# Stick-breaking attention: both heads' scores on row halves, weighted values on column halves, and a new order of the stage

## The reference, cut to what matters

```
q = rms_norm_2(heads(q), q_gain); k = rms_norm_2(heads(k), k_gain); v = heads(v)
z = einsum('bhtd,bhsd->bhts', q, k) * scale              # scale = 1/8
mask = s_pos[None, :] < t_pos[:, None]
log_stay = where(mask, log_sigmoid(-z), 0.0)
later = cumsum(log_stay, axis=3, reverse=True) - log_stay # sum over later keys
weight = where(mask, exp(log_sigmoid(z) + later), 0.0)
out = einsum('bhts,bhsd->bhtd', weight, v)
```

## Time and profile before

| | us |
|---|---|
| device time, median of 3 runs | 2165.52 (2161.07 to 2167.31) |
| span of the profiled execution | 2161.0 |
| stick-breaking attention, first z to first matmul that closes the output projection | 1477.9 to 1757.6 |
| PE busy in the span | 2096.7 |
| DVE / ACT / POOL busy | 907.0 / 737.8 / 811.5 |

### The profile page before, as it was taken

One profiled execution on the slowest core, in us unless ns is written; L12 is line 12 of the kernel. 1 busy time (PEld: TensorE's weight loads), 2 busy tenths in 40 slices (PEclk: granted clock), 3 DMA queues, 4 the chain that ended last, 5 costly groups with the idle time before them and its releaser, 6 DMA issues.

```text
span 2161.0 us, 25942 instructions
## 1 busy us (share of the span) xinstructions
PE 2096.7 (97%) x8990; PEld 1648.1 (76%) x8990; DVE 907.0 (42%) x1040; ACT 737.8 (34%) x967; POOL 811.5 (38%) x328
## 2 busy tenths in 40 slices
PE   7999989999998999999999999999999989999999
PEld 4677758888885777787888888886777768888887
DVE  6455454333224343343234443225777764444300
ACT  3333342233223333334233323224454543333211
POOL 3222244444444433332444444443222224444443
PEclk8999999999998999999999999999999999999999
DMA  4111112223221222221222223222111112222322
GB/s 148 49 49 51 58 57 97 97 97 108 94 90 59 94 86 69 97 82 64 93 96 97 97 97 106 94 83 70 47 49 39 49 49 88 97 97 97 106 94 92
DMA packets 48137, 177.31 MB, mean 82 GB/s; under 512 B 5472, under 2 KB 6240, under 8 KB 48096
## 3 DMA queue, kind: packets, MB, share of 16 engines
q1 hardware_dynamic: 46224, 172.62, 23.5%
q10 hardware_dynamic: 1872, 4.13, 0.6%
HBM read 174.63 MB, written 2.10 MB: 82 GB/s over the span
## 4 chain that ended last, share of the span: by engine, by line
PE 86%; DVE 8%; issue 3%; ACT 3%; DMA 0%; DVEq 0%; ACTq 0%; SPq 0%
PE B L261 23%; PE B L262 23%; PE B L266 23%; PE B L678 2%; PE B L668 1%; PE B L672 1%; PE B L669 1%; DVE SPL L1611 1%; PE B L529 1%; PE B L560 1%; PE B L277 1%; PE B L279 1%; PE B L278 1%; PE B L813 1%; PE B L775 1%
## 5 line engine op out<-in xcount | busy, mean ns | idle before, releaser
L408 POOL TENSOR_TENSOR WL<-RAW,WH 128x1024 fp32r<-128x1024 f32 (+1 forms) x304 | 781.7, 2572 | 1326.3 <-PE B L266 861.4
L261 PE MATMUL B<-HH,WH 128*128 128x512 f32 x1624 | 642.3, 396 | 5.7 <-DVE QT L1348 5.7
L262 PE MATMUL B<-HL,WH 128*128 128x512 f32 x1624 | 633.7, 390 | 0.0
L249 ACT CAST WH<-RAW 128x1024 fp32r<-128x1024 f32 (+1 forms) x304 | 333.8, 1098 | 639.3 <-PE B L262 584.6
L266 PE MATMUL B<-HH,WL 128*128 128x512 f32 x1624 | 401.4, 389 | 0.0
L261 PEld LDWEIGHTS B<-HH,WH 128*128 128x128 f32 x1624 | 306.0, 188 | 78.6 <-issue 9.3
L262 PEld LDWEIGHTS B<-HL,WH 128*128 128x128 f32 x1624 | 305.9, 188 | 65.2 <-issue 2.6
L266 PEld LDWEIGHTS B<-HH,WL 128*128 128x128 f32 x1624 | 304.8, 188 | 63.3
L261 PE MATMUL B<-MH,WH 128*128 128x512 f32 x462 | 182.5, 395 | 0.0
L262 PE MATMUL B<-ML,WH 128*128 128x512 f32 x462 | 182.5, 395 | 0.0
L1274 DVE TENSOR_TENSOR U<-B,RB 128x512 f32<-128x512 f32 x66 | 45.6, 691 | 309.4 <-PE B L266 309.4
(11 more groups left out here) (233 smaller groups left out, 2343.8 us busy)
## 6 DMA issues: line engine op xcount, KB each, us to landing
RAW<-in_w_small SPq DMA_DIRECT2D x256, 512.0 KB, 3.2
RAW<-in_w_large SPq DMA_DIRECT2D x48, 704.0 KB, 4.0
X<-in_x_t ACTq DMA_DIRECT2D x4, 512.0 KB, 8.6
out_t<-X SPq DMA_DIRECT2D x8, 256.0 KB, 5.2
DECAY<-in_decay ACTq DMA_DIRECT2D x4, 256.0 KB, 2.5
INV<-in_inv_counts SPq DMA_DIRECT2D x1, 512.0 KB, 9.2
BIAS<-in_bias SPq DMA_DIRECT2D x1, 256.0 KB, 9.1
CS<-in_cos SPq DMA_DIRECT2D x1, 256.0 KB, 9.1
```

The lines of the kernel that those rows point to most:

```text
L249: act.copy(WH[u.s][:, 0:chunks, :], RAW[u.s][:, 0:chunks, :]).then_inc(s_hi, 1)
L261: pe.matmul(bank, wh[:, c, :], xh[:, k0 + c, :], start=(start and c == 0), stop=False)
L262: mm = pe.matmul(bank, wh[:, c, :], xl[:, k0 + c, :], start=False, stop=False)
L408: pool.tensor_tensor(WL[u.s][:, 0:chunks, :], RAW[u.s][:, 0:chunks, :], WH[u.s][:, 0:chunks, :].bitcast(F32), ALU.subtract).then_inc(s_lo, 1)
```

## The change

The two heads are computed together. `z` now issues all eight strips in one go, head 0 and head 1 in turn, each on its 64 rows of the array, into B2, B3 and one half of B4 for head 0, B5, B6 and the other half of B4 for head 1. `values` issues both heads in turn too: v is kept once (VN3, no zeros), a head's 64 columns of it are loaded and its result goes to partitions 64h to 64h+63 of B7. The memset of VZ3 on GpSimd goes. The new values wait for the weights of both heads, and one semaphore count stands for both.

The stage has a new order. On TensorE: unit q, values of pair a - 1, z of pair a, unit k, the first part of unit v (16 matmuls), the sums of head 0, the last 8 matmuls of unit v, the sums of head 1, the transposes. In the last stage both started output units stand ahead of the sums, and head 1's sums get banks of their own (B5, B6, B7). DVE and ACT are reordered to match.

z and values on TensorE:

```
-                def z(h):
-                    hd = a * 2 + h
+                def z():
                     pe.wait_ge(b_qk, a * 2 + 2)
...
+                    if not first_a:
+                        pe.wait_ge(b_arg, a * 6)
+                    for h, sb_, bank, at in ((0, 2, 4, 0), (1, 0, 5, 0), (0, 0, 2, 0), (1, 1, 6, 0), (0, 1, 3, 0),
+                                             (1, 2, 4, 256), (0, 3, 3, 384), (1, 3, 6, 384)):
                         w = t_width(sb_)
+                        r = slice(64 * h, 64 * h + 64)
+                        if h == 1 and bank == 4:
+                            pe.wait_ge(b_z, a * 8 + 1)
+                        pe.matmul(B[bank][:, at:at + w], KT3[r, ap, P * sb_:P * sb_ + P], QT3[r, ap, P * sb_:T],
+                                  start=True, stop=True).then_inc(b_z, 1)
...
+                def values(a, ap):
+
+                    pe.wait_ge(b_w, a * 2 + 2)
+                    pe.wait_ge(b_v, a + 1)
+                    pe.wait_ge(s_m, a + M_BASE[4])
                     for sb_ in range(TB):
                         w = t_width(sb_)
-                        mm = pe.matmul(B[7][:, P * sb_:T], VZ3[:, ap, h, sb_, :],
...
+                        for h in range(2):
+                            mm = pe.matmul(B[7][64 * h:64 * h + 64, P * sb_:T], VN3[:, ap, sb_, 64 * h:64 * h + 64],
+                                           ZS[:, h, T_AT[sb_]:T_AT[sb_] + w], start=(sb_ == 0),
+                                           stop=(sb_ == TB - 1), skip_group_check=True)
```

The sums' waits and the stage on TensorE (`high_part` and `low_part` are the two halves of `use_unit`):

```
                     if h == 0:
-                        pe.wait_ge(b_zs, hd * 4 + 8)
+                        pe.wait_ge(b_zs, a * 8 + 8)
+                    elif j is not None:
+                        pe.wait_ge(b_arg, hd * 3)
                     else:
-                        pe.wait_ge(b_arg, hd * 3)
...
+                        pe.wait_ge(s_m, a + M_BASE[4])
+                        places = LAST_AT
...
-                if a is not None:
-                    z(0)
...
-                        values(1, a - 1, 1 - ap)
-                    z(1)
+                    if not first_a:
+
+                        values(a - 1, 1 - ap)
+                    z()
                     if j is None:
                         start_out(0)
+                        start_out(1)
+                        later(0)
+                        later(1)
+                        values(a, ap)
...
                     head_mean(0)
-                if a is not None:
-                    later(0)
-                if j is not None:
                     pe.wait_ge(b_qs, jj * 2 + 1)
-                    use_unit(pe, u + 2, B[0][:], DC, HH, HL)
+                    high_part(pe, u + 2, B[0][:], DC, HH, HL)
+                    if a is not None:
+                        later(0)
+                    low_part(pe, u + 2, B[0][:], DC, HH)
                     head_mean(1)
...
+                    if a is not None:
+                        later(1)
```

take_z on VectorE, the copy of v on ScalarE, the memset on GpSimd:

```
+                    full, rest = ((2, 3), (5, 6))[h]
+                    for n, (sb_, bank, at) in enumerate(((0, full, 0), (1, rest, 0), (3, rest, 384), (2, 4, 256 * h))):
                         w = t_width(sb_)
-                        dve.wait_ge(b_z, hd * 4 + (4 if n else 1))
+                        if h == 0 and n < 2:
+                            dve.wait_ge(b_z, a * 8 + (8 if n else 3))
...
+                def copy_v():
+
+                    act.wait_ge(b_vt, jj + 1)
+                    act.copy(VN3[:, jp, :, :], B[1][:].rearrange("p (t d) -> p t d", t=TB)).then_inc(b_v, 1)
...
-                if first == U_SB + 2:
-
-                    pool.wait_ge(s_unit, U_SB)
-                    pool.memset(VZ3[:], 0.0).then_inc(b_zero, 1)
```

More of the change, by code:

```diff
@@ L257, in use_unit, with high_part @@
                 return
-            wh, wl = WH[u.s], WL[u.s]
+            high_part(pe, u, bank, chunks, xh, xl, k0, start)
+            low_part(pe, u, bank, chunks, xh, k0, stop)
+        def high_part(pe, u, bank, chunks, xh, xl, k0=0, start=True):
+            wh = WH[u.s]
             pe.wait_ge(s_hi, u.index + 1)
@@ L865, in stick_stage @@
                     mm.then_inc(b_vt, 1)
-                if a is not None:
-                    values(0, a, ap)
-                    if j is None:
-                        values(1, a, ap)
             stick_stage((0, 0), 0, None, None)
@@ L1147, in stick_stage, with exp_term @@
                 first = isinstance(jj, int) and jj == 0
+                first_a = isinstance(a, int) and a == 0
+                def exp_term(h):
+                    hd = a * 2 + h
+                    act.wait_ge(b_abs, hd + 1)
+                    act.activation(LG[:, h, :], LG[:, h, :], ACT.Exp).then_inc(b_ex, 1)
                 def log_term(h):
-                    hd = a * 2 + h
-                    act.wait_ge(b_na, hd + 1)
-                    act.activation(LG[:, h, :], LG[:, h, :], ACT.Exp).then_inc(b_lg, 1)
-                    act.wait_ge(b_lg, hd * 2 + 1)
+                    act.wait_ge(b_ex, a * 2 + h + 1)
                     act.activation(LG[:, h, :], LG[:, h, :], ACT.Ln, bias=1.0).then_inc(b_lg, 1)
@@ L1159, in softplus_hi @@
                     act.wait_ge(b_sp, hd * 2 + 1)
-                    if not (isinstance(a, int) and a == 0):
+                    if not first_a:
                         act.wait_ge(b_later, hd * 3 - 3)
@@ L1204, in stick_stage @@
                     rn(1, jj, first)
-                    split_hi(act, u + 4, DC)
+                    copy_v()
                 if a is not None:
                     weights(1)
-                if j is not None:
-                    act.wait_ge(b_vt, jj + 1)
-                    if first:
-                        act.wait_ge(b_zero, 1)
-                    if not (isinstance(jj, int) and jj < 2):
-                        act.wait_ge(b_pv, jj * 2 - 2)
-                    for h in range(2):
-                        act.copy(VZ3[:, jp, h, :, 64 * h:64 * h + 64],
-                                 B[1][:].rearrange("p (t d) -> p t d", t=TB)[:, :, 64 * h:64 * h + 64])\
-                           .then_inc(b_v, 1)
-                elif a is not None:
-                    mixed_hi(a)
+                    if j is None:
+                        mixed_hi(a)
             def rn(n, jj, first):
@@ L1617, in exponent @@
                     dve.wait_ge(b_sp, hd * 2 + 2)
-                    for n, (bank, at, w) in enumerate(((2, 0, 512), (3, 512, 512), (4, 1024, 256))):
+                    banks = (5, 6, 7) if j is None and h else (2, 3, 4)
+                    for n, (bank, at, w) in enumerate(zip(banks, (0, 512, 1024), (512, 512, 256))):
                         dve.wait_ge(b_later, hd * 3 + n + 1)
@@ L1641, in norm_qk @@
                                              op1=ALU.mult).then_inc(b_qk, 1)
-                if a is not None:
-                    take_z(0)
                 if j is not None:
@@ L1647, in stick_stage @@
                 if a is not None:
-                    if j is None:
+                    if not (isinstance(a, int) and a == 0):
                         mixed_lo(a - 1)
+                    take_z(0)
+                    take_z(1)
                     softplus(0)
-                    softplus_lo(0)
-                    if j is not None and not (isinstance(a, int) and a == 0):
-                        mixed_lo(a - 1)
-                    take_z(1)
                 if j is not None:
@@ L1657, in stick_stage @@
                 if a is not None:
+                    softplus_lo(0)
                     softplus(1)
-                    exponent(0)
-                    softplus_lo(1)
                 if j is not None:
                     norm_qk(0)
+                if a is not None:
+                    softplus_lo(1)
+                    exponent(0)
+                if j is not None:
                     wait_unit(dve, u + 2)
```

87 lines of the change are left out of this document (33 added, 54 removed).

## The result

| | before | after |
|---|---|---|
| device time, median of 4 runs each on one chip | 2166.41 (2161.07 to 2167.36) | 2174.64 (2173.88 to 2175.30) |
| ratio | | 1.0048, 95% 1.0034 to 1.0061 |
| span of the profiled execution | 2161.0 | 2173.5 |
| one stage in the loop (six) | 35.05 | 37.46 |
| first stage with attention | 35.37 | 34.83 |

The account below looks back on a forecast made before the run. TensorE was taken as nearly full, other engines setting only its waits. Loop +6.9, last stage -3.0 and clock +10.2 gave +14.1 us; 2165.5 + 14 = 2179.5 us, own range 2172 to 2190, whole range 2148 to 2207.

Parts of the forecast that it names:

- z and values on halves: TensorE's attention matmuls: the two heads overlap in part, 2.75 us for either block, saving 3.7 us of work per stage.
- Rival 1: The two heads' halves don't overlap, +44 us, 2209, or only one kind does, about +30, 2195; chance 0.20.
- The order: New stage order: head 0's sums start near 13.45 us after z starts, with 0.5 us of wait or so.
- Two WL passes in the way: GpSimd passes hold VectorE's normalised q and SPL; TensorE waits some 5.9 us; period 36.2, +1.15 per stage, +6.9 in all.
- The clock: The long TensorE wait brings the lower clock level in every loop stage: 1.7 us each, six times, +10.2 us.
- First and last stage: Attention's end stages: no difference in the first, -3.0 us in the last (36.2 to 33.2).
- The sum: All terms on the profiled execution: +14.1 us, 2161.0 becomes 2175.1.
- The last term of the forecast: Step from profiled span to median: the median of the runs lies 4.5 us above the span.
- the signs that I named: Period near 37.9 us, wait 5 to 6.5, one SPL near 3.7, normalised q near 3, PEclk 0.50 for 3 to 5.
- Rival 2: GpSimd's passes miss VectorE's work, or VectorE keeps the port: wait about 1.2 us, -28 us, 2138; chance 0.15.

Follow-up runs that it names:

- filled wait: The changed kernel with 20 extra matmuls of 512 columns on TensorE ahead of head 1's sums, where it idled; 2158.16 us, ratio 0.9962 to the kernel before.
- One cast late: The changed kernel with only the WH cast of unit k's weights moved behind head 0's weights on ScalarE; 2154.30 us, ratio 0.9944 to the kernel before.
- heads apart: The changed kernel with z and values issued for all strips of head 0, then all of head 1; 2195.76 us, ratio 1.0135 to the kernel before.
- both casts late: The changed kernel with both WH casts of the next stage moved behind head 0's weights on ScalarE; 2131.32 us, ratio 0.9831 to the kernel before.

## Why the prediction was right, and where its terms were off

**z and values on halves**: mis-sized. I took 2.75 us each, from records that start in order; they took 2.36 and 2.31, full overlap. The "up to 2x" of the Trainium skill (TensorEngine Tiling (Array Packing), Theoretical Speedup) was the better price here: the trace agrees, 4.67 us for what took 9.20. Rival 1 fell, and its own sizes too, since even head by head a pair costs 3.75 and 3.86 us and not 4.6.

**The order**: right. Counted from z, head 0's sums stood at 13.45 with a wait of 0.5; they started at 1684.61 - 1671.52 = 13.1 with 0.43.

**Two WL passes in the way**: right in mechanism and place. I had the normalised q held until 18.5 (18.6 measured), SPL of head 1 from 19.2 to 23.0 (18.6 to 22.2), head 1's sums at 24.65 with a wait of 5.9 (23.8, with 4.93). Moving both casts, or one, shows it as cause. The period without the lower level I put at 36.2, +1.15 us per stage; filled wait has 35.00, so it is -0.05. Of the difference 0.8 is the sums' earlier start and 0.4 the shorter values. The rule of the Trainium skill that the prediction named (SBUF — State Buffer, Who interferes with whom) has the lock; the trace agrees, and adds that the two engines take turns.

**The clock**: mis-sized the other way. I took 1.7 us, one stretch with full work; there were two, and the cost is 2.46 per stage by filled wait. I had the upper bound of 2.8 (half of 5.43 is rather 2.7) from the second place in the earlier trace rows, and took the lower one because its wait was the likeness; but that wait was 2.6 us and this one 4.9. One cast late, with 2.8 us of wait, shows one stretch again, in five stages of six. But the wait's length alone doesn't fix the number: 2.8 and 3.5 us were followed by one stretch or two, and heads apart had one behind 4.9 us (the stage from 1674.18, period 39.44) where its others had two (40.1 to 40.5). A second stretch made a stage some 0.9 to 1.2 us longer. The prediction also read the trace of before too simply when it found 0.50 behind each long wait: behind 3.23 us at 71.59 and 2.42 us at 1508.21 it has none.

**First and last stage**: 0 and -3.0 forecast, -0.5 and -4.8 measured. In the last stage values began 2.1 us behind its mark, where I had counted some 3.3 for both heads' weights, took 0.4 us less, and head 1's SPL ended at z + 16.7 instead of 17.3; the end, partly at the lower level, took 0.4 more.

**The sum**: +6.9 - 3.0 + 10.2 = +14.1 forecast; in the attention of the profiled execution it was -0.3 - 0.5 - 4.8 + 14.8 = +9.2, within rounding the +9.1 above. Two errors, 7 us too much for the passes and 4.6 too little for the clock, partly cancelled, and that is luck. So is the nearness of the span, 2173.5 against 2175.1 forecast: the 3.0 us ahead of the attention, which the sum doesn't hold, stand in for most of the rest. The last term of the forecast was off too: the median lies 1.1 us above after's span, not 4.5 as before, since before's profiled execution was shorter than most of its runs and after's was the longest of its four. So the medians differ by 8.2 and not by 14. Of the signs that I named, the wait (4.93 us for 5 to 6.5) and z (2.36 for 2.5 to 2.9) missed narrowly and the time at the lower level (6.8 us a stage for 3 to 5) by more; the period, SPL and the normalised q came as said.

Rival 2 (the passes miss DVE's work) I put at 2138 us. That kernel is both casts late, 2131.3: its size was near, and its deciding point, which of WL and SPL asks first, is where the 43 us lie.

The 2.4 us per stage add up: z and values fell by 4.5 us, the waits grew by 4.1, the clock costs 2.5, the three units take 17.4 us instead of 16.7 (unit v, now cut in two by the sums, 6.1 instead of 5.5), and head 0's sums 2.8 instead of 3.1.

## What to carry to other kernels

A saving on the bounding engine is only as good as the wait that it exposes: count the path of the other engines to the next thing it needs, and look for what runs on GpSimd at that time, since a GpSimd pass there holds VectorE work on two SBUF operands for the pass's length. Move the instruction that starts the pass, or cut the pass into shorter instructions; the first was worth 43 us here, the second 30, 22 of them in the attention. And price a wait on TensorE with the clock that follows it: here 4.9 us idle in every stage cost 2.5 us more, 2.8 us idle one stretch at the lower level in most stages and two in some, and 1.3 us none. Two kernels with the same wait can differ by that alone.

## What the runs showed of the hardware that I had not expected

- Matmuls of two heads on different halves, issued in turn, run fully beside each other: in values their fp32 records start 7 ns apart, in z the first two do, and a pair costs what one cost (2.36 us against 2.35, 2.31 against 2.25).
- Issued head by head, the second head's first matmul started before earlier queued ones of the first head's half, by the records' lengths and columns (3.75 and 3.86 us for a pair). The Trainium skill (TensorE: Matmul & The Clock Gate, The mechanism) has matmuls as "strict FIFO, no reordering"; where it and this record differ, I go by the record.
- Halved GpSimd passes next to VectorE work took 1.96, 1.72, 2.52 and 1.27 us, one behind the other, with VectorE's two operations between them: the engines alternate, one instruction each.
- Extra work made the kernel faster: 20 matmuls per stage in an idle place saved 16.5 us.
- The same wait in the same kernel was followed by 3.41 us at the lower level in some stages and 6.83 in others (3.5 us of wait, three stages of each, period about 35.1 and 36.15).
